# Writing the expert slots' results by token row instead of by slot row in a hybrid diffusion step

## Chip, cores and metric

The kernel is written for one Trainium2 chip and runs on one of its cores. The metric is the time of an execution on the device in microseconds (us); several executions are timed and the median is taken.

## What is computed

One layer of a diffusion backbone over 128 context and 512 latent tokens of width 1024, in fp32. A convolution branch and an mLSTM branch are merged, projected and added to the input. Then comes the part that this change is about, a mixture of experts:

```python
gl = x @ w_rg + b_rg                       # 4 groups: the top one is taken
el = (x @ w_re + b_re)[.., chosen group]   # 4 experts in it: the top two are taken
weights = gp_sel * topv                    # two weights per token
act = silu(x @ w_e_gate[e]) * (x @ w_e_up[e])      # 16 experts, 1024 -> 256
out[token] += weight * (act @ w_e_down[e])         # 256 -> 1024
x = x + gate2 * out;  y = rms_norm(x, norm_final_g)
```

The two results of a token are weighted and added after all experts have run.

## The kernel before

The 640 tokens are 5 tiles (`NT`) of 128 rows; with two experts each there are 1280 pairs of token and expert. The routing sorts the pairs into *slots* of 128 rows (`CAP`): slots 0 to 15 take the first 128 pairs of each expert, further slots what is left over, and the kernel runs an odd number of slots that it reads from the data (17 with these inputs). A slot that is not full has empty rows, whose token index lies outside the table, so that an indirect DMA skips them.

Each engine has its own instruction stream and they meet in semaphores. Matmuls take fp32 in two parts, a rounded high part and the rest (`_h`, `_l`), so every weight tile is halved once by ScalarE (ACT, high) and once by VectorE or GpSimd (low). For slot b the streams do the following; slots alternate between two sets of buffers s.

- SyncE (SP) loads the weights on its DMA queue: gate and up (1 MB each) of slot b+2 once TensorE has finished gate and up of slot b, and the down matrix (1 MB) of slot b+1 once the down product of b-1 is finished.
- ACT, function `slot`: high part of the activation of b-1, of x of b+1 (`x_high`), `store_y(s, b-2)`, high parts of gate and up of b+1 (L1516), silu of b, high part of the down matrix of b (L1511, semaphore `d_hi`), then the left half of the result of b-1 from PSUM into `yy` (L1560).
- VectorE (DVE): low part of the activation of b-1 and of x of b+1, low part of gate of b+1 (L1977), the product `act_` of b (L2021), low part of up of b+1 (L1977), right half of the result of b-1 into `yy` (L2002).
- TensorE (PE): turn `act_` of b-1 and the gathered x of b+1, gate and up of b, down of b-1, in this order.
- GpSimd (POOL), function `experts_pool`: for slot b the indirect DMA that gathers the x rows of slot b+3 (L609), then the low part of the down matrix of b (L631), which waits for `d_hi`. For b from 11 on the slot number comes from data: `counted_gather` first copies the column of indices to a fixed place, with a tiny operation (`carry`, L605) before and after the copy, and then issues the DMA.

The result of slot b leaves by `store_y`, a plain DMA of the whole tile on ACT's queue, to row b*128 of `y_d`. `y_left` and `y_right` of slot b wait on `y_st` until the store of b-2 has landed, because they write the same buffer. The rows of `y_d` that no slot may write are filled beforehand by ten plain copies of input on SP's queue (L689), early in the kernel. After the last slot POOL waits until all stores have landed and gathers for each of the 5 tiles the two rows of each token (`ya`, `yb`, L653, ten indirect DMAs by `row_i`). The last stage takes the tiles in order: ACT weighs `ya` (L1613), DVE adds the weighted `yb`, applies gate and residual and the final norm (L2045 to L2057), SP stores.

Of the kernel before, what the change touches and what calls it, by code (L numbers as in the profile page):

```python
# [10 lines left out]
P = 128  # L11
# [26 lines left out]
FILL = (NS - NE) // 2  # L38
# [117 lines left out]
def build(nc, a, out):  # L156
# [13 lines left out]
    y_d = nc.dram_tensor("y_d", [NS * CAP, D], F32, kind="Internal").ap()  # L170
# [114 lines left out]
    row_i = place("row_i", R0 + 3 * K + 64, [P, NT, 2], I32)  # L285
# [6 lines left out]
    ob = place("ob", 59 * K, [P, 2, NT, 2, NS], BF16)  # L292
# [16 lines left out]
    slot_b = place("slot_b", CV0 + 4 * K, [P, 2], I32)  # L309
    ah = place("ah", CV0 + 2 * K, [P, 2, P], F32R)  # L310
    al = place("al", CV0 + 3 * K, [P, 2, P], F32R)
    tick = place("tick", CV0 + 4 * K + 64, [P, 3], I32)
# [71 lines left out]
    picked, hots, slots, tables = sem("picked"), sem("hots"), sem("slots"), sem("tables")  # L384
    e_hi, e_lo, d_hi, d_lo, e_used = (sem(n) for n in ("e_hi", "e_lo", "d_hi", "d_lo", "e_used"))
    slot_set = sem("slot_set")
# [4 lines left out]
    y_act, y_dve = sem("y_act"), sem("y_dve")  # L391
# [92 lines left out]
    def routing(dve, then):  # L484
# [31 lines left out]
        dve.tensor_tensor(picks[:, :, :], full(13), full(14), ADD).then_inc(picked, 1)  # L516
# [43 lines left out]
        then(dve.tensor_copy(r1[:, 16, 0:2 * NS], psum[:, 6, 0:2 * NS]))  # L560
# [4 lines left out]
        then(dve.scalar_tensor_tensor(out=pair_of(6), in0=pair_of(2), scalar=float(CAP), in1=pair_of(4), op0=MUL, op1=ADD))  # L565
        dve.tensor_copy(row_i[:, :, :].rearrange("p t i -> p i t"), pair_of(6))
# [31 lines left out]
    def experts_pool(pool):  # L598
# [62 lines left out]
    def _(sp):  # L661
# [14 lines left out]
        for g in LOAD_ORDER:  # L676
# [54 lines left out]
        sp.wait_ge(y_st[0], 16 * FILL)  # L731
        sp.wait_ge(y_st[1], 16 * FILL)
# [11 lines left out]
        down_weights(0, 2 * pairs, by_table(2 * pairs), False)  # L744
        for t in range(NT):
# [48 lines left out]
    def _(pe):  # L794
# [351 lines left out]
        pe.wait_ge(picked, 1)  # L1146
# [9 lines left out]
        pe.wait_ge(hots, 1)  # L1156
        for n in range(2 * NT):
            mm = pe.matmul(psum[:, 6, 0:2 * NS], oa[:, n // NT, n % NT, :], ob[:, n // NT, n % NT, :, :],
                           start=(n == 0), stop=(n == 2 * NT - 1))
# [22 lines left out]
        def down(s, b, first=False):  # L1182
# [5 lines left out]
            if not first:  # L1188
                pe.wait_ge(y_act, b)
                pe.wait_ge(y_dve, b)  # L1190
# [37 lines left out]
    def _(act):  # L1228
# [326 lines left out]
        def y_left(s, j, b, first=False):  # L1555

            act.wait_ge(e_used, b + 1)
            if not first:
                act.wait_ge(y_st[s], 16 * (j + FILL))
            act.activation(yy[:, s, 0:512], psum[:, 5, :], ACT.Copy).then_inc(y_act, 1)  # L1560
# [10 lines left out]
        act.wait_ge(y_st[0], 16 * FILL)  # L1571
        act.wait_ge(y_st[1], 16 * FILL)
# [3 lines left out]
        def slot(b, s, u, last=False):  # L1576
# [7 lines left out]
            if early >= 2:  # L1584
                store_y(s, b - 2)
# [20 lines left out]
        store_y(1, 2 * pairs - 1)  # L1606
        y_left(0, pairs, 2 * pairs)
        store_y(0, 2 * pairs)
# [16 lines left out]
    def _(dve):  # L1625
# [460 lines left out]
```

## Time and profile before

| | us |
|---|---|
| median of 3 runs (lowest, highest) | 810.46 (809.5, 812.64) |
| the profiled execution: its own time | 812.8 |
| the profiled execution: span of its profile | 810.9 |
| mean granted TensorE clock over it | 0.942 of full speed |
| busy: PE, DVE, ACT, POOL | 686.9, 527.4, 348.0, 185.0 |

PE, PEld, DVE, ACT and POOL are the matmuls, the weight loads of TensorE, VectorE, ScalarE and GpSimd; ACTq and SPq are DMAs that ACT and SP issue. L12 is line 12 of the kernel. A row of the timeline gives start, duration, engine, line, operation, output<-input, and in brackets how long the engine was idle before it and what ended that. The span has these stretches: up to 578 us the layer's other parts and the routing, 585 to 768 us the 17 slots, 768 to 811 us the last stage.

### The profile page before, as it was taken

What the parts mean: (1) busy time and instruction counts of PE and PEld (TensorE: products, weight loads), DVE (VectorE), ACT (ScalarE), POOL (GpSimd) and SP (SyncE); (2) the same over time, 40 slices, a digit from 0 to 9 for tenths busy, and PEclk for the clock granted to TensorE, in tenths of its full rate; (3) what the DMA queues carried; (4) which work ended last, traced back from release to release, by engine and by line L of the source; (5) the groups of instructions that cost most, each with busy time, mean ns of one, the idle gap of its engine ahead of it and who ended that gap; (6) DMA issues with size and microseconds to landing.
All of it is one profiled execution on the core that took longest, in us unless ns stands there. A gap on an engine that the chain in (4) does not pass through costs nothing.

```text
span 810.9 us, 11103 instructions
## 1 busy us (share of the span) xinstructions
PE 686.9 (85%) x4391; PEld 608.7 (75%) x4391; DVE 527.4 (65%) x764; ACT 348.0 (43%) x467; POOL 185.0 (23%) x83
## 2 busy tenths in 40 slices
PE   2799999999888998899999999996189998989700
PEld 1599999999777888788889998884177777767600
DVE  2447999999376555633355554565857777788557
ACT  4542123433133343334375121036077767777432
POOL 3004222233000000000000000000147766797250
PEclk9889999999799999999999999998599999999955
DMA  9934144663305533623342436224299999999473
GB/s 318 349 108 144 53 156 158 233 232 108 107 14 113 103 32 105 121 90 104 104 152 90 138 103 232 78 106 157 96 315 366 367 367 380 395 391 374 160 272 122
DMA packets 80452, 150.22 MB, mean 185 GB/s; under 512 B 11669, under 2 KB 63217, under 8 KB 73713
## 3 DMA queue, kind: packets, MB, share of 16 engines
q1 hardware_dynamic: 62192, 121.25, 44.7%
q10 hardware_dynamic: 14320, 17.77, 6.6%
q0 software_dynamic: 3888, 10.49, 3.6%
q8 instruction: 35, 0.57, 0.3%
q14 instruction: 17, 0.13, 0.1%
HBM read 138.31 MB, written 20.09 MB: 195 GB/s over the span
## 4 chain that ended last, share of the span: by engine, by line
PE 40%; DVE 25%; POOL 11%; issue 9%; DMA 8%; ACT 5%; ACTq 2%; POOLq 0%; DVEq 0%
DVE psum L1714 13%; PE psum L843 13%; PE psum L1129 7%; POOL down_l L631 6%; PE psum L1087 4%; POOL xg L609 3%; PE psum L796 2%; DMA w_raw<-in_w_in 2%; PE psum L859 2%; PE psum L1020 1%; PE psum L939 1%; PE psum L986 1%; DMA cn<-in_state_n 1%; DMA xg<-h_d,slot_b 1%; DMA out_new_n<-cout 1%
## 5 line engine op out<-in xcount | busy, mean ns | idle before, releaser
L843 PE MATMUL psum<-hh,w_h 128*128 128x320 f32 x608 | 145.2, 320 | 2.9 <-ACT modrow L1403 1.9
L843 PE MATMUL psum<-hh,w_l 128*128 128x320 f32 x608 | 139.0, 310 | 0.0
L843 PE MATMUL psum<-hl,w_h 128*128 128x320 f32 x608 | 139.0, 310 | 0.0
L609 POOL DMA_INDIRECT xg<-h_d,slot_i x14 | 31.0, 2217 | 387.6 <-DVE slot_i L563 378.0
L1714 DVE SCALAR_TENSOR_TENSOR psum<-conv,taps,psum 128x760 f32<-128x760 f32 x106 | 107.6, 1015 | 3.6
L1977 DVE TENSOR_TENSOR w_l<-w_raw,w_h 128x2048 fp32r<-128x2048 f32 x34 | 94.9, 2794 | 19.8 <-ACT w_h L1516 19.8
L843 PEld LDWEIGHTS psum<-hh,w_h 128*128 128x128 f32 x608 | 100.2, 190 | 9.5 <-issue 6.4
L843 PEld LDWEIGHTS psum<-hl,w_h 128*128 128x128 f32 x608 | 102.3, 189 | 0.0
L843 PEld LDWEIGHTS psum<-hh,w_l 128*128 128x128 f32 x608 | 102.1, 189 | 0.0
L631 POOL TENSOR_TENSOR down_l<-down_raw,down_h 128x2048 fp32r<-128x2048 f32 x16 | 75.0, 4687 | 48.0 <-ACT down_h L1511 47.9
L788 POOL TENSOR_TENSOR w_l<-w_raw,w_h 128x2048 fp32r<-128x2048 f32 x9 | 41.7, 4637 | 150.2 <-ACT w_h L1234 150.2
L1516 ACT ACTIVATE w_h<-w_raw 128x2048 fp32r<-128x2048 f32 x34 | 65.2, 1923 | 18.4 <-DMA w_raw<-in_w_e_up 14.6
L1234 ACT ACTIVATE w_h<-w_raw 128x2048 fp32r<-128x2048 f32 x24 | 45.9, 1910 | 48.2 <-DMA w_raw<-in_w_in 31.2
L458 PE MATMUL psum<-w_h,xh 128*128 128x512 f32 x136 | 55.0, 405 | 0.0
L459 PE MATMUL psum<-w_h,xl 128*128 128x512 f32 x136 | 53.4, 393 | 0.0
L1511 ACT ACTIVATE down_h<-down_raw 128x2048 fp32r<-128x2048 f32 x17 | 32.6, 1916 | 24.2 <-DMA down_raw<-in_w_e_down 24.2
L1834 DVE TENSOR_TENSOR num<-psum,inter 128x129 f32<-128x129 f32 x32 | 9.4, 293 | 38.0 <-ACT inter L1322 38.0
L1868 DVE TENSOR_TENSOR w_l<-w_raw,w_h 128x2048 fp32r<-128x2048 f32 x13 | 29.6, 2281 | 6.3 <-ACT w_h L1234 6.3
L464 PE MATMUL psum<-w_l,xh 128*128 128x512 f32 x136 | 33.6, 389 | 0.0
L1322 ACT ACTIVATE inter<-psum,tokg 128x129 f32<-128x129 f32 x32 | 11.9, 371 | 50.5 <-PE psum L946 50.5
L1129 PE MATMUL psum<-w_h,mh 128*128 128x512 f32 x80 | 31.4, 393 | 1.1 <-DVE mrg L1929 1.1
L1129 PE MATMUL psum<-w_h,ml 128*128 128x512 f32 x80 | 31.2, 390 | 0.0
(335 smaller groups left out, 1314.6 us busy)
## 6 DMA issues: line engine op xcount, KB each, us to landing
w_raw<-in_w_ada SPq DMA_DIRECT2D x20, 1024.0 KB, 7.9
w_raw<-in_w_in SPq DMA_DIRECT2D x20, 1024.0 KB, 11.8
w_raw<-in_w_e_gate SPq DMA_DIRECT2D x17, 1024.0 KB
w_raw<-in_w_e_up SPq DMA_DIRECT2D x17, 1024.0 KB, 10.2
down_raw<-in_w_e_down SPq DMA_DIRECT2D x17, 1024.0 KB, 11.8
y_d<-yy ACTq DMA_DIRECT2D x17, 512.0 KB, 8.1
y_d<-in_x_sample SPq DMA_DIRECT2D x10, 512.0 KB, 7.5
w_more<-in_w_ada SPq DMA_DIRECT2D x4, 1024.0 KB, 11.9
```

What stands on the lines that cost most here:

```text
L458: pe.matmul(dst, lh, rh, start=(k == 0), stop=False)
L459: pe.matmul(dst, ll, rh, start=False, stop=False)
L464: mm = pe.matmul(dst, lh, rl, start=False, stop=(k == len(terms) - 1))
L609: pool.indirect_dma_start(out=xg[:, s, :], out_offset=None, in_=h2_d, in_offset=bass.IndirectOffsetOnAxis(ap=index, axis=0), bounds_check= ...
L631: pool.tensor_tensor(down_l[s][:, 0, :], down_raw[s][:, 0, :], down_h[:, s, :].bitcast(F32), SUB).then_inc(d_lo, 1)
L788: pool.tensor_tensor(w_l[:, g % RING, :], w_raw[:, g % RING, :], w_h[:, g % RING, :].bitcast(F32), SUB).then_inc(lo_done, 1)
L843: mm = pe.matmul(psum[:, p + q, 0:HALF], w, r[:, k, q * HALF:(q + 1) * HALF], start=(k == 0 and x == 0), stop=(k == KT - 1 and x == 2))
L1129: mm = pe.matmul(psum[:, n % 4, :], l, r, start=(k == 0 and x == 0), stop=(k == KT - 1 and x == 2))
L1234: act.activation(w_h[:, g % RING, :], w_raw[:, g % RING, :], ACT.Copy).then_inc(hi_done, 1)
L1516: act.activation(w_h[:, 2 * s + c, :], w_raw[:, 2 * s + c, :], ACT.Copy).then_inc(e_hi, 1)
L1714: ins = dve.scalar_tensor_tensor(out=after, in0=src, scalar=w, in1=before, op0=MUL, op1=ADD)
L1977: dve.tensor_tensor(w_l[:, 2 * s + c, :], w_raw[:, 2 * s + c, :], w_h[:, 2 * s + c, :].bitcast(F32), SUB).then_inc(e_lo, 1)
```

## The change

`y_d` becomes a table of 2*640 rows: row i*640 + token holds the result for the token's i-th expert. The routing makes a second table, `pair_i`, beside the one for the gather: per slot and row the row of `y_d`. It comes from a third plane of `ob` in the same matmuls (78 instead of 52 columns). `store_y` is gone; POOL scatters the rows of slot b-2 by indirect DMA, between its gather of b+3 and its low part of b. The ten filling copies and the waits on them are gone. The last stage's ten indirect gathers become ten plain loads on SP's queue, after POOL has seen all scatters land. The semaphores of the two halves of a result become one (`y_out`).

```diff
@@ routing, DVE @@
+        dve.tensor_scalar(ob[:, 1, :, 2, :], obh[:, 1, :, :], float(NT), None, MUL)
...
-        then(dve.tensor_copy(r1[:, 16, 0:2 * NS], psum[:, 6, 0:2 * NS]))
+        then(dve.tensor_copy(r1[:, 16, 0:3 * NS], psum[:, 6, 0:3 * NS]))
...
-        then(dve.scalar_tensor_tensor(out=pair_of(6), in0=pair_of(2), scalar=float(CAP), in1=pair_of(4), op0=MUL, op1=ADD))
-        dve.tensor_copy(row_i[:, :, :].rearrange("p t i -> p i t"), pair_of(6))
+        then(dve.scalar_tensor_tensor(out=r1[:, 6, 0:NS], in0=r1[:, 16, 2 * NS:3 * NS], scalar=float(P), in1=r1[:, 17, 0:NS],
+                                      op0=MUL, op1=ADD))
+        dve.tensor_scalar(pair_i[:, :], r1[:, 6, 0:NS], float(EMPTY * P), None, ADD)
@@ experts_pool @@
+        def scatter(s, index):
+
+            pool.indirect_dma_start(out=y_d, out_offset=bass.IndirectOffsetOnAxis(ap=index, axis=0), in_=yy[:, s, :],
+                                    in_offset=None, bounds_check=2 * T - 1, oob_is_err=False).then_inc(y_st[s], 16)
+
+        def known_scatter(b):
+
+            pool.wait_ge(y_out, 2 * b + 2)
+            scatter(b % 2, pair_i[:, b:b + 1])
+
+        def counted_scatter(s, b):
+
+            pool.wait_ge(y_out, 2 * b + 2)
+            carry(2, pair_i[:, 0:1])
+            pool.tensor_copy(pair_b[:, s:s + 1], pair_i[:, bass.ds(b, 1)]).then_inc(pair_set, 1)
+            pool.wait_ge(pair_set, b - (POOL_LOOP_AT - 3))
+            carry(3, pair_b[:, s:s + 1])
+            scatter(s, pair_b[:, s:s + 1])
...
         for b in range(POOL_LOOP_AT):
             known_gather(b + 3)
+            if b >= 2:
+                known_scatter(b - 2)
             low(b % 2, b)
...
                 counted_gather(1 - s, b + 3)
+                counted_scatter(s, b - 2)
                 low(s, b)
         counted_gather(0, 2 * pairs)
+        counted_scatter(1, 2 * pairs - 5)
         low(1, 2 * pairs - 3)
+        counted_scatter(0, 2 * pairs - 4)
         low(0, 2 * pairs - 2)
+        counted_scatter(1, 2 * pairs - 3)
         low(1, 2 * pairs - 1)
-        pool.wait_ge(y_st[0], 16 * (pairs + 1 + FILL))
-        pool.wait_ge(y_st[1], 16 * (pairs + FILL))
-        carry(2, row_i[:, 0, 0:1])
-        for t in range(NT):
-            for i, buf in enumerate((ya, yb)):
-                pool.indirect_dma_start(out=buf[:, t, :], out_offset=None, in_=y_d,
-                                        in_offset=bass.IndirectOffsetOnAxis(ap=row_i[:, t, i:i + 1], axis=0),
-                                        bounds_check=NS * CAP - 1).then_inc(yg_in[t], 16)
+        counted_scatter(0, 2 * pairs - 2)
+        counted_scatter(1, 2 * pairs - 1)
+        counted_scatter(0, 2 * pairs)
+        pool.wait_ge(y_st[0], 16 * (pairs + 1))
+        pool.wait_ge(y_st[1], 16 * pairs)
+        pool.tensor_tensor(tick[:, 0:1], pair_i[:, 0:1], pair_i[:, 0:1], ADD).then_inc(y_all, 1)
@@ SP @@
-            n = g - 2 * NRAW_ADA
-            if 0 <= n < NS - NE:
-                sp.dma_start(y_d[(NE + n) * CAP:(NE + n + 1) * CAP, :],
-                             a["x_sample"][0, (n % (NT - 1)) * P:(n % (NT - 1) + 1) * P, :]).then_inc(y_st[n % 2], 16)
...
+        sp.wait_ge(y_all, 1)
+        for t in range(NT):
+            for i, buf in enumerate((ya, yb)):
+                sp.dma_start(buf[:, t, :], y_d[i * T + t * P:i * T + (t + 1) * P, :]).then_inc(yg_in[t], 16)
@@ ACT @@
-        def store_y(s, b):
-            act.wait_ge(y_act, b + 1)
-            act.wait_ge(y_dve, b + 1)
-            rows = slice(b * CAP, (b + 1) * CAP) if isinstance(b, int) else bass.ds(b * CAP, CAP)
-            act.dma_start(y_d[rows, :], yy[:, s, :]).then_inc(y_st[s], 16)
...
-            if early >= 2:
-                store_y(s, b - 2)
...
-        store_y(1, 2 * pairs - 1)
         y_left(0, pairs, 2 * pairs)
-        store_y(0, 2 * pairs)
```

## Rows read from the trace of the kernel before

**Rows 1.** The page: GB/s in 40 slices of 20.3 us.

```profile
GB/s 318 349 108 144 53 156 158 233 232 108 107 14 113 103 32 105 121 90 104 104 152 90 138 103 232 78 106 157 96 315 366 367 367 380 395 391 374 160 272 122
```

**Rows 2.** The page, DMA queues: packets, MB, share of 16 engines.

```profile
...
q10 hardware_dynamic: 14320, 17.77, 6.6%
q0 software_dynamic: 3888, 10.49, 3.6%
```

**Rows 3.** Waits between 610 and 737 us: total, times, longest.

```profile
...
ACT down_h L1511 <- DMA down_raw<-in_w_e_down: 19.2, 12, 2.1
PEld psum L796 <- DVE act L2021: 14.0, 10, 2.2
```

**Rows 4.** Windows: busy of PE, PEld, DVE, ACT, POOL; clock, DMA share, GB/s.

```profile
...
623.20:634.50 11.30, 9.53 (x47) 7.76 (x46) 8.22 (x7) 7.66 (x9) 7.51 (x3) 1.00 1.00 395
634.50:644.50 10.00, 9.62 (x48) 7.83 (x47) 8.13 (x7) 7.70 (x9) 7.55 (x3) 1.00 0.94 352
```

**Rows 5.** Timeline, slots with fixed numbers, POOL, DVE and ACT.

```profile
...
609.77 4.72 POOL L631 TENSOR_TENSOR down_l<-down_raw,down_h 128x2048 fp32r<-128x2048 f32 x1 [5.00 <-ACT down_h L1511]
...
684.52 4.62 POOL L631 TENSOR_TENSOR down_l<-down_raw,down_h 128x2048 fp32r<-128x2048 f32 x1 [2.54 <-ACT down_h L1511]
688.00 3.29 DVE L1977 TENSOR_TENSOR w_l<-w_raw,w_h 128x2048 fp32r<-128x2048 f32 x1 [1.01 <-ACT w_h L1516]
689.30 2.88 POOL L609 DMA_INDIRECT xg<-h_d,slot_i  x1 [0.16 <-issue]
691.22 0.41 DVE L2021 TENSOR_TENSOR act<-psum,sil 128x256 f32<-128x256 f32 x1
691.55 2.28 DVE L1977 TENSOR_TENSOR w_l<-w_raw,w_h 128x2048 fp32r<-128x2048 f32 x1
692.87 1.92 ACT L1511 ACTIVATE down_h<-down_raw 128x2048 fp32r<-128x2048 f32 x1 [1.85 <-DMA down_raw<-in_w_e_down]
...
694.88 4.62 POOL L631 TENSOR_TENSOR down_l<-down_raw,down_h 128x2048 fp32r<-128x2048 f32 x1 [2.70 <-ACT down_h L1511]
...
705.21 4.62 POOL L631 TENSOR_TENSOR down_l<-down_raw,down_h 128x2048 fp32r<-128x2048 f32 x1 [2.67 <-ACT down_h L1511]
```

**Rows 6.** Timeline, slots with counted numbers, POOL, DVE and PE.

```profile
...
720.37 2.25 POOL L605 TENSOR_TENSOR tick<-slot_i 128x1 int32<-128x1 int32 x1
722.56 0.18 POOL L623 COPY slot_b<-slot_i 128x1 int32 x1
722.82 2.33 POOL L605 TENSOR_TENSOR tick<-slot_b 128x1 int32<-128x1 int32 x1
725.30 1.05 POOL L609 DMA_INDIRECT xg<-h_d,slot_b  x1 [0.15 <-issue]
726.39 4.66 POOL L631 TENSOR_TENSOR down_l<-down_raw,down_h 128x2048 fp32r<-128x2048 f32 x1
728.78 4.43 DVE L1977 TENSOR_TENSOR w_l<-w_raw,w_h 128x2048 fp32r<-128x2048 f32 x1 [1.17 <-ACT w_h L1516]
...
737.01 4.65 POOL L631 TENSOR_TENSOR down_l<-down_raw,down_h 128x2048 fp32r<-128x2048 f32 x1
...
742.61 1.07 PE L464 MATMUL psum<-down_l,ah 128*128 128x512 f32 x4
```

**Rows 7.** Timeline from the last result on.

```profile
...
767.66 0.69 DVE L2002 COPY yy<-psum 128x512 f32<-128x512 f32 x1 [1.39 <-PE psum L464]
...
771.36 0.19 POOL L605 TENSOR_TENSOR tick<-row_i 128x1 int32<-128x1 int32 x1 [10.24 <-DMA y_d<-yy]
772.14 1.05 POOL L653 DMA_INDIRECT ya<-y_d,row_i  x1 [0.59 <-issue]
...
778.75 1.15 ACT L1613 ACTIVATE ya<-ya,wgt 128x1024 f32<-128x1024 f32 x1 [10.51 <-DMA yb<-y_d,row_i]
```

**Rows 8.** DMA issues: count, KB each, median us to landing.

```profile
...
y_d<-yy ACTq DMA_DIRECT2D x17, 512.0 KB, 8.1
x<-in_x_prompt SPq DMA_DIRECT2D x1, 512.0 KB, 3.4
```

**Rows 9.** Timeline of the routing, DVE.

```profile
...
576.63 0.35 DVE L553 TENSOR_SCALAR ob<-obh,tokcol 128x260 bf16<-128x260 f32 x1
```

More of the change, by code:

```diff
@@ L37 @@
 NS = NB + NB % 2
-FILL = (NS - NE) // 2
 EMPTY = 16
@@ L169, in build @@
     mod2_d = nc.dram_tensor("mod2_d", [2, 4 * D], F32, kind="Internal").ap()
-    y_d = nc.dram_tensor("y_d", [NS * CAP, D], F32, kind="Internal").ap()
+    y_d = nc.dram_tensor("y_d", [2 * T, D], F32, kind="Internal").ap()
     ident = keep("ident", [P, P])
@@ L284, in build @@
     wgt = place("wgt", R0 + 3 * K, [P, NT, 2])
-    row_i = place("row_i", R0 + 3 * K + 64, [P, NT, 2], I32)
+    pair_i = place("pair_i", R0 + 3 * K + 256, [P, NS], I32)
     slot_i = place("slot_i", R0 + 3 * K + 128, [P, NS], I32)
@@ L291, in build @@
     oa = place("oa", 56 * K, [P, 2, NT, P], BF16)
-    ob = place("ob", 59 * K, [P, 2, NT, 2, NS], BF16)
+    ob = place("ob", 59 * K, [P, 2, NT, 3, NS], BF16)
     obh = place("obh", 62 * K, [P, 2, NT, NS])
@@ L309, in build @@
     slot_b = place("slot_b", CV0 + 4 * K, [P, 2], I32)
+    pair_b = place("pair_b", CV0 + 4 * K + 32, [P, 2], I32)
     ah = place("ah", CV0 + 2 * K, [P, 2, P], F32R)
     al = place("al", CV0 + 3 * K, [P, 2, P], F32R)
-    tick = place("tick", CV0 + 4 * K + 64, [P, 3], I32)
+    tick = place("tick", CV0 + 4 * K + 64, [P, 4], I32)
     bg2 = place("bg2", R0 + 5 * K, [P, 2, D])
@@ L383, in build @@
     rt_x, rt_exp, rt_pe = sem("rt_x"), sem("rt_exp"), sem("rt_pe")
-    picked, hots, slots, tables = sem("picked"), sem("hots"), sem("slots"), sem("tables")
+    hots, slots, tables = sem("hots"), sem("slots"), sem("tables")
     e_hi, e_lo, d_hi, d_lo, e_used = (sem(n) for n in ("e_hi", "e_lo", "d_hi", "d_lo", "e_used"))
-    slot_set = sem("slot_set")
+    slot_set, pair_set = sem("slot_set"), sem("pair_set")
     xg_in = [sem(f"xg_in{i}") for i in range(2)]
@@ L390, in build @@
         sem(n) for n in ("gu_done", "sil_done", "act_done", "at_done", "a_hi", "a_lo"))
-    y_act, y_dve = sem("y_act"), sem("y_dve")
+    y_out, y_all = sem("y_out"), sem("y_all")
     y_st = [sem(f"y_st{i}") for i in range(2)]
@@ L515, in routing @@
                                    plane(hot, GE).unsqueeze(2).to_broadcast([P, NT, NG, GE]), MUL))
-        dve.tensor_tensor(picks[:, :, :], full(13), full(14), ADD).then_inc(picked, 1)
+        dve.tensor_tensor(picks[:, :, :], full(13), full(14), ADD).then_inc(hots, 1)
         dve.wait_ge(rt_pe, 1)
@@ L730, in _ @@
         sp.wait_ge(h2_st, 16 * NT)
-        sp.wait_ge(y_st[0], 16 * FILL)
-        sp.wait_ge(y_st[1], 16 * FILL)
         down_weights(0, 0, own(0), True)
@@ L1144, in _ @@
         mm.then_inc(lg_done, 1)
-        pe.wait_ge(picked, 1)
+        pe.wait_ge(hots, 1)
         for t in range(NT):
@@ L1154, in _ @@
         mm.then_inc(rt_pe, 1)
[L1156 to L1159, printed above, removed]
+        pe.wait_ge(hots, 2)
+        for i in (1, 0):
+            for t in range(NT):
+                mm = pe.matmul(psum[:, 6, 0:(2 + i) * NS], oa[:, i, t, :], ob[:, i, t, 0:2 + i, :],
+                               start=(i == 1 and t == 0), stop=(i == 0 and t == NT - 1))
         mm.then_inc(rt_pe, 1)
@@ L1188, in down @@
             if not first:
-                pe.wait_ge(y_act, b)
-                pe.wait_ge(y_dve, b)
+                pe.wait_ge(y_out, 2 * b)
             for q in range(2):
@@ L1558, in y_left @@
             if not first:
-                act.wait_ge(y_st[s], 16 * (j + FILL))
-            act.activation(yy[:, s, 0:512], psum[:, 5, :], ACT.Copy).then_inc(y_act, 1)
-        def store_y(s, b):
-            act.wait_ge(y_act, b + 1)
-            act.wait_ge(y_dve, b + 1)
-            rows = slice(b * CAP, (b + 1) * CAP) if isinstance(b, int) else bass.ds(b * CAP, CAP)
-            act.dma_start(y_d[rows, :], yy[:, s, :]).then_inc(y_st[s], 16)
+                act.wait_ge(y_st[s], 16 * j)
+            act.activation(yy[:, s, 0:512], psum[:, 5, :], ACT.Copy).then_inc(y_out, 1)
         for q in range(2):
@@ L1570, in _ @@
         act.wait_ge(h2_st, 16 * NT)
-        act.wait_ge(y_st[0], 16 * FILL)
-        act.wait_ge(y_st[1], 16 * FILL)
         load_mod(act, 3, bg2, gate2_in)
@@ L2000, in y_right @@
             if not first:
-                dve.wait_ge(y_st[s], 16 * (j + FILL))
-            dve.tensor_copy(yy[:, s, 512:D], psum[:, 6, :]).then_inc(y_dve, 1)
+                dve.wait_ge(y_st[s], 16 * j)
+            dve.tensor_copy(yy[:, s, 512:D], psum[:, 6, :]).then_inc(y_out, 1)
         for c in range(2):
```

## The prediction, made before the change was run

> **What bounds the kernel now.** I read the page first, for where the DMA engines are full, then the queues and the waits of the expert slots, then one slot after the other in the timeline, and the last stage row by row. In the expert slots the DMA rate stands at 366 to 395 GB/s for seven slices in a row, against less than 235 GB/s in nearly every slice before it [rows 1]. So bytes saved there can be worth time, and bytes saved elsewhere (the ten filling copies, early in the kernel) are not: I cost their removal at nothing, because the slices in which they run (102 to 175 us, the sixth to ninth) carry 156 to 233 GB/s.
>
> A slot moves 3 x 1.05 MB of weights, a store of 0.524 MB and the gathered rows. That empty rows move no bytes can be read off the software queue: its 10.49 MB are 2560 rows of 4 KB, exactly two rounds of the 1280 real rows (x once, results once), while its 3888 packets are 27 indirect DMAs of 128 + 16 [rows 2]. An empty row costs a packet and no data. So the gather is 5.24/17 = 0.31 MB a slot, the slot 3.98 MB, and at 375 GB/s, the middle of the slices, 10.6 us. POOL's work on the down matrix comes once a slot; nine periods from 609.77 to 705.21 are 10.60 us each [rows 5]. The two agree, and ACT waits for weights in every slot [rows 3].
>
> But DMA is not alone there. PE has 9.5 us of work in a slot of 11.3 [rows 4], and it waits for the product `act_` of DVE [rows 3], which stands behind DVE's low part of the gate weights. That row takes 3.29 us where the like one after it takes 2.28, since POOL holds something that both need: POOL's 4.62 us on the down matrix end at 689.14, and DVE's operation, begun at 688.00, ends 2.15 us after that. The same holds the other way round: the gather issued at 689.30 takes 2.88 us and ends 0.9 us after DVE's [rows 5], while one that meets no such operation takes 1.05 [rows 6]. So POOL's and DVE's big subtractions exclude each other, and an indirect DMA cannot begin inside DVE's. The slots alternate between long ones, with DMA share 1.00, and short ones of about 10 us with 0.94 [rows 4]: DMA ends the wait in the one, this chain nearly does in the other.
>
> **Part 1, fixed slots (2 to 10): the bytes.** The stores go from 17 x 0.524 = 8.91 MB to 5.24 MB, 3.67 MB less, 9.8 us of DMA time at 375 GB/s or 0.58 us a slot. The slot's DMA time falls from 10.6 to 10.0 us. Nine periods: at most -5.4 us.
>
> **Part 2, fixed slots: the scatter on POOL.** In the row order of one slot, from the start T of the down operation: it ends at T+4.62; DVE's gate part runs to T+6.77; the gather, blocked by it, ends at T+7.66 (684.52 to 692.18). `act_` takes DVE to T+7.0, and the up part runs from T+7.03 to T+9.3 [rows 5]. Now the scatter is queued behind the gather. It wants to start at T+7.8, inside the up part, so it is held until T+9.3 and ends 0.9 later, at T+10.2; the next down operation starts at T+10.36. Today that operation starts at T+10.36 as well (694.88), let go by ACT's `down_h`, which waited for DMA [rows 5]. So the scatter fits, but it sets a floor: low part, gate part, `act_`, up part and scatter in a ring give 10.36 us. The trace has no scatter; its bounds are 1.05 us (free) and 2.88 (blocked), and I take the blocked one, as the gather in the same place. The period goes from 10.60 to 10.4: 9 x 0.2 = -2 us. If the long slots stay long, because a load's latency and not the rate makes them, nothing is gained and the short ones lose 0.1: +0.7.
>
> At this place the Trainium skill speaks against the change: its page SBUF — State Buffer, section "Who interferes with whom", has software-made DMAs (POOL's) share a port with DVE that DMAs of ACT and SP do without, and a store is moved from the second kind to the first. The gather's 2.88 us against 1.05 agrees. The same section infers that a two-input DVE operation holds up only POOL's reads, so that the making of descriptors would go on beside it; by that the floor would be gone (a rival below).
>
> **Part 3, counted slots (11 to 13).** Here POOL has no gap: the two tiny operations take 2.25 and 2.33 us because each ends with a DVE weight operation, the copy 0.18 and the gather 1.05; the down operation of one slot follows that of the last after 10.6 us without idle time [rows 6]. The counted scatter adds a tiny operation (0.19 when nothing blocks it, as the one at 771.36 [rows 7]), the copy 0.18, another 0.19, gaps of 0.3 and 1.05 for the DMA: 1.9 us free, and up to 2.3 more for each tiny operation that meets DVE. It comes when DVE works from PSUM, before its next gate part (728.78, 2.4 us after the down operation's start [rows 6]), so I take 1.9. Three times that is 5.7 us. What is late next: the down operation of slot 13, which ends at 741.67 and which PE's last pass of down needs at 742.61 [rows 6]. That cover is 0.9 us, so PE is late by 4.8. Behind it on POOL stand the last gathers, late by 3.8 after two scatters, which fits under the same delay. Afterwards POOL has idle gaps for the other scatters. +4.8 us; the low end is +2 (the tiny operations of the gather are then blocked for a shorter time, because DVE is ahead), the high end +9.
>
> **Part 4, the end.** Today the last result is in `yy` at 768.35, the store, POOL's tiny operation and two gathers follow, and ACT starts on the first tile at 778.75: 10.4 us [rows 7]. Afterwards: tiny operation, copy, tiny operation and gaps 0.9; the scatter from issue to landing between 1.05 + 2.8 = 3.9 (the plain store took 2.8 to 771.36) and 5.3 (two gathers issued 1.3 us apart took 6.6 to 778.75 [rows 7]), 4.3 since the last slot holds few rows; POOL's signal to SP 0.5; two plain loads of 0.5 MB, of which one took 3.4 us [rows 8] and the second adds up to 1.4: 4.2. Sum 9.9, so -0.5 us, with bounds -1.6 and +1.5. The ten loads are 5.2 MB, 2.8 us a tile at 375 GB/s. I cost them at nothing after the first tile, since the DVE operations and not the gathers pace the tiles today; without that cover they would show as waits of ACT.
>
> **Part 5, small ones.** The third plane of `ob` is one more DVE operation before the first gather, half the size of the one of 0.35 us [rows 9]: 0.25, and the wider copy 0.05. +0.3 us, on the path. `pair_i` costs what `row_i` did. ACT loses 17 DMA issues, each beside other work: nothing. The renamed semaphores: nothing. The fifteen first scatters must land before `yy` is written again: a store of this size lands in 8.1 us [rows 8], and a scatter issued at T+7.8, held for 1.5 us, has until about T+20 us. Hidden, by some 2 us.
>
> **Sum.** -2.0 + 4.8 - 0.5 + 0.3 = +2.6 us. The profiled execution had its own time 812.8 us (span 810.9, 1.9 around it), so 815.4 on its scale; it lies 2.3 above the median 810.46 of the runs shown, so the median should be 813.1. Within 0.5% (4.05 us) a measurement of this kernel can hardly tell a change, so this is "no change", on its upper side. By itself this case reaches from 809.5 to 816.
>
> **Rivals.**
> *Slower: the counted scatter meets DVE's lock* (0.22). If in slots 11 to 13 one tiny operation of each scatter falls into DVE's gate or up part, it costs 2.2 us more, 3 x 2.2 = 6.6 at most, of which I expect most: 819. For it: every tiny operation in that loop today meets one [rows 6]. Against it: the scatter comes behind both weight operations. It decides from a scatter section of 2.4 us instead of 1.9, since then DVE's gate part is there first.
> *Slower: scatters land late* (0.10). Behind the gather in the same queue, with all DMA engines busy, the scatter could take 11 us and more. Then ACT and DVE wait to write `yy`, and everything after them in ACT's order (the high parts) is late. Past 10 us to landing each of 12 slots would lose up to 0.5: 816 to 819. For it: the cover is thin. Against it: a plain store took 8.1 [rows 8].
> *No lock for the scatter* (0.12). Then part 2 has no floor and the period falls to the 10.0 us of DMA: -5.4 + 4.8 - 0.5 + 0.3 = -0.8, 809.7. This is what the inference of the Trainium skill's page SBUF — State Buffer, section "Who interferes with whom", would give. Against it: the gather was held.
> *Faster: the bytes decide everywhere* (0.13). Full relief in the fixed slots, -5.4, the counted slots at their low end, +2, the tail at its low end, -1.6, and +0.3: -4.7, 805.8. It decides once the fixed period is under 10.1 and POOL's added time in the counted slots under 2 us a chain. For it: DMA share near 1 in the long slots [rows 4]. Against it: POOL without a gap in the counted ones [rows 6].
> The forecast keeps 0.43. That the change doesn't remove the bytes I exclude by the software queue's count.
>
> **Chances.** Faster by over 0.5%: the faster rival 0.13, and 0.03 from the edges of the forecast and the no-lock case: 0.16. Slower: 0.22 + 0.10, and 0.09 from the forecast's upper edge: 0.41. The rest, 0.43. The range 806 to 819 leaves out about one in ten on either side.
>
> **What the profile would show.** The software queue at 3888 packets or near and 10.49 MB, and 17.77 - 8.91 = 8.9 MB in the queue that held the stores. In slots 2 to 10, a period of 10.4 us and scatter rows of about 2.9, ending 0.9 us after a DVE weight operation. In slots 11 to 13, down operations 12 to 12.5 us apart, and PE waiting for POOL's `down_l` in slot 14. From the last `yy` to ACT's first tile 9.9 us. What would make it wrong: a landing time of the scatter far from 8 us, a scatter whose work on POOL grows with something that the gather's does not, or DVE and POOL falling into another order once POOL is late, as each slot's order is a race of about 1 us.

## The result, and the profile of the changed kernel

The changed kernel has a median of 818.48 us (8 executions, 811.33 to 821.61) beside 810.21 us (8 executions, 807.69 to 813.89) for the kernel before on the same chip: a ratio of 1.0091, 95% interval 1.0057 to 1.0124. That is slower by 0.9%, about 7.4 us, more than the 0.5% below which no change can be told. The ratio, here and below, is estimated from the undisturbed executions of both kernels and is not exactly the quotient of the medians beside it, which are over all executions (here they stand 8.3 us apart). The profiled execution took 815.61 us, with a span of 813.8; since it lies 2.9 us under its median and the profiled one of before 2.6 over its own, the two spans differ by only 2.9 us. So I read them stretch by stretch and not by their ends.

Busy tenths of POOL in 40 slices (20.3 us each), from the page of the kernel before:

```profile
POOL 3004222233000000000000000000147766797250
```

The page of the changed kernel: busy tenths of POOL and GB/s in 40 slices, and the DMA queues; they answer to [rows 1, 2].

```profile
POOL 3004222233000000000000000000269999999700
...
GB/s 317 348 105 145 52 104 108 170 140 104 107 19 107 118 44 81 179 86 100 153 60 167 123 28 233 104 78 155 141 354 364 368 352 346 371 271 348 107 266 123
...
q10 hardware_dynamic: 11872, 8.86, 3.8%
q0 software_dynamic: 4896, 10.50, 3.5%
```

The bytes did go: 8.86 MB stay in the queue that held the stores, 17.77 before. The rate in the expert slots fell as well, from a range of 366 to 395 GB/s to one of 346 to 371 with one slice of 271, and POOL is busy for 90% or more in seven slices in a row, before in one. The DMA engines have been relieved, and POOL has become the busy one.

POOL in nine slots with fixed numbers: groups of its instructions (count, busy us, mean ns, idle time before them and what ended it). The first list is of before and has the down operations of slots 1 to 9, the second is of after and has those of slots 1 to 10.

```profile
L631 POOL TENSOR_TENSOR down_l<-down_raw,down_h 128x2048 fp32r<-128x2048 f32 x9 | 41.7, 4631 | 28.8 <-ACT down_h L1511 28.8
```

```profile
L652 POOL TENSOR_TENSOR down_l<-down_raw,down_h 128x2048 fp32r<-128x2048 f32 x10 | 46.6, 4659 | 1.7 <-ACT down_h L1534 1.5
...
L632 POOL DMA_INDIRECT y_d<-yy,pair_i x9 | 21.9, 2432 | 2.8 <-issue 2.8
```

Of the 28.8 us for which POOL stood still before, 5.0 stand ahead of slot 1's operation, and the 2.67 ahead of slot 10's aren't among them [rows 5]; so between the starts of the two POOL waited 26.5 us for ACT. After, 1.3 of the 1.5 us stand ahead of slot 1's operation, and POOL waited 0.24 us in the nine slots. The scatter with its gap (21.9 + 2.8) ate the slack. One such slot of after, POOL and DVE, which answers to [rows 5]:

```profile
679.63 4.63 POOL L652 TENSOR_TENSOR down_l<-down_raw,down_h 128x2048 fp32r<-128x2048 f32 x1
684.42 2.90 POOL L611 DMA_INDIRECT xg<-h_d,slot_i  x1 [0.16 <-issue]
687.63 2.30 POOL L632 DMA_INDIRECT y_d<-yy,pair_i  x1 [0.31 <-issue]
689.95 4.62 POOL L652 TENSOR_TENSOR down_l<-down_raw,down_h 128x2048 fp32r<-128x2048 f32 x1
```

```profile
682.90 3.53 DVE L1988 TENSOR_TENSOR w_l<-w_raw,w_h 128x2048 fp32r<-128x2048 f32 x1 [1.00 <-ACT w_h L1539]
...
686.76 2.28 DVE L1988 TENSOR_TENSOR w_l<-w_raw,w_h 128x2048 fp32r<-128x2048 f32 x1
```

DVE's up part ends at 689.04 and the scatter at 689.93, 0.9 us later, as the gather does after the gate part (686.43 and 687.32). The down operation follows at once.

The slots with counted numbers on POOL, which answer to [rows 6]:

```profile
705.35 2.25 POOL L607 TENSOR_TENSOR tick<-slot_i 128x1 int32<-128x1 int32 x1
707.54 0.18 POOL L625 COPY slot_b<-slot_i 128x1 int32 x1
707.80 2.33 POOL L607 TENSOR_TENSOR tick<-slot_b 128x1 int32<-128x1 int32 x1
710.27 1.06 POOL L611 DMA_INDIRECT xg<-h_d,slot_b  x1
711.36 0.20 POOL L607 TENSOR_TENSOR tick<-pair_i 128x1 int32<-128x1 int32 x1
711.49 0.19 POOL L644 COPY pair_b<-pair_i 128x1 int32 x1
711.76 0.19 POOL L607 TENSOR_TENSOR tick<-pair_b 128x1 int32<-128x1 int32 x1
712.49 1.02 POOL L632 DMA_INDIRECT y_d<-yy,pair_b  x1 [0.54 <-issue]
713.54 4.58 POOL L652 TENSOR_TENSOR down_l<-down_raw,down_h 128x2048 fp32r<-128x2048 f32 x1
...
726.31 6.00 POOL L652 TENSOR_TENSOR down_l<-down_raw,down_h 128x2048 fp32r<-128x2048 f32 x1
...
737.65 2.82 POOL L632 DMA_INDIRECT y_d<-yy,pair_b  x1 [0.54 <-issue]
740.50 4.55 POOL L652 TENSOR_TENSOR down_l<-down_raw,down_h 128x2048 fp32r<-128x2048 f32 x1
```

The down operations stand 12.8 (700.77 to 713.54), 12.8 and 14.2 us apart, 10.6 before. The scatter section takes 2.2 us (711.36 to 713.54). The third distance is longer since one down operation met DVE's weights (6.00 us) and one scatter did (2.82). The three together are 39.7 us, 7.9 more than before. In slots 14 and 15 the scatters' tiny operations meet DVE too (2.25 us at 745.01, 2.25 and 2.33 from 753.82 on), but before the change POOL was idle for 4.3 and 5.7 us there, and PE waits 0.24 us for slot 15's operation and not at all for slot 14's.

What PE waited for between 705 and 768 us, from the waits (total, times, longest), first before, then after; from the down operation of slot 10 to the last `yy` the numbers are the same:

```profile
PE psum L796 <- DVE act L2021: 2.2, 3, 1.0
PE psum L796 <- DMA xg<-h_d,slot_b: 1.7, 2, 1.5
...
PE psum L458 <- DVE al L1994: 1.2, 1, 1.2
```

```profile
PE psum L464 <- POOL down_l L652: 5.2, 4, 3.1
PE psum L819 <- DVE act L2032: 2.9, 3, 1.3
PE psum L458 <- DVE al L2005: 1.3, 1, 1.3
```

PE's waits are 5.1 us before and 9.4 after, and the new one is for POOL's `down_l`, four times (1.55, 0.31, 3.13 and 0.24 us, for slots 11, 12, 13 and 15). The second thing is what PE does behind such waits. Timeline of PE, after:

```profile
718.18 1.21 PE L464 MATMUL psum<-down_l,ah 128*128 128x512 f32 x4 [1.55 <-POOL down_l L652]
720.68 0.70 PE L819 MATMUL psum<-ident,act 128*128 128x128 f32 x2 [1.28 <-DVE act L2032]
...
724.16 0.63 PE L459 MATMUL psum<-w_h,xl 128*128 128x512 f32 x1
724.59 0.63 PE L458 MATMUL psum<-w_h,xh 128*128 128x512 f32 x1
...
726.65 0.39 PE L459 MATMUL psum<-w_h,xl 128*128 128x512 f32 x1
726.88 0.39 PE L458 MATMUL psum<-w_h,xh 128*128 128x512 f32 x1
```

After two waits of 1.55 and 1.28 us the matmuls begin 0.43 us apart, until 726.3, and then 0.23 apart: TensorE's clock stood at the lower level, 1.2 GHz, instead of 2.4. The windows (last three columns: granted clock, DMA share, GB/s) give its mean in the stretch, first before, then after:

```profile
713.50:726.30 12.80, 10.33 (x51) 8.32 (x50) 10.85 (x10) 10.46 (x13) 12.39 (x7) 1.00 0.97 385
...
759.80:772.60 12.80, 6.47 (x27) 4.55 (x25) 4.43 (x5) 3.66 (x5) 1.97 (x3) 0.97 0.21 84
```

```profile
713.50:726.30 12.80, 9.96 (x37) 7.79 (x35) 11.52 (x8) 9.49 (x10) 11.86 (x10) 0.74 0.91 333
...
759.80:772.60 12.80, 10.45 (x38) 7.75 (x36) 4.43 (x5) 3.65 (x5) 9.08 (x9) 0.87 0.22 87
```

The loss in a window is its length times what the clock lacks of 1.00, less what falls into a wait. The first window gives 12.8 x 0.26 = 3.3 us. In windows of 1 us the lower level stands from 719.7 to 726.5, so 1.0 us of it lies in the wait that ends at 720.68, and 2.8 us are lost. The second window gives 12.8 x 0.13 = 1.7 us (lower level from 767.5 to 770.9). The 0.97 of before counts for nothing: the clock falls only at about 771.8, behind its last `yy` at 768.35.

Between the down operation of slot 10 and the last `yy` lie 63.1 us before (705.21 to 768.35) and 71.8 after (700.77 to 772.58): 8.7 us more. The waits give 4.3 of them and the clock 4.5, together 8.8. The same reckoning fits all twelve profiles of this case: that stretch less PE's waits and less the loss by the clock is 57.3 to 58.8 us in each.

The end, which answers to [rows 7]:

```profile
771.89 0.69 DVE L2013 COPY yy<-psum 128x512 f32<-128x512 f32 x1 [2.67 <-PE psum L464]
...
773.93 1.00 POOL L632 DMA_INDIRECT y_d<-yy,pair_b  x1 [0.54 <-issue]
776.63 0.18 POOL L680 TENSOR_TENSOR tick<-pair_i 128x1 int32<-128x1 int32 x1 [1.71 <-DMA y_d<-yy,pair_b]
...
777.22 0.43 SPq L767 DMA_DIRECT2D yb<-y_d  x1
...
781.69 1.15 ACT L1624 ACTIVATE ya<-ya,wgt 128x1024 f32<-128x1024 f32 x1 [9.30 <-DMA yb<-y_d]
```

From the last `yy` (772.58) to ACT's first tile are 9.1 us, 10.4 before. From there to the end are 32.1 us in both. The last scatter needs 2.7 us from issue to landing, and ACT starts 4.5 us after the issue of the second load (777.22).

### The profile page after: what moved, and what is told of

The parts are those of the page before. It is cut to its first block, busy times and chain, and to the rows that moved or that the text cites. A ratio compares the mean times of both kernels' runs of the same rounds, so it can differ in the third digit from the quotient of the medians.

```text
span 813.8 us, 11100 instructions
## 1 busy us (share of the span) xinstructions
PE 691.2 (85%) x4391; PEld 611.9 (75%) x4391; DVE 535.2 (66%) x765; ACT 348.2 (43%) x467; POOL 218.5 (27%) x114
## 3 DMA queue, kind: packets, MB, share of 16 engines
q10 hardware_dynamic: 11872, 8.86, 3.8%
q0 software_dynamic: 4896, 10.50, 3.5%
HBM read 133.07 MB, written 14.85 MB: 182 GB/s over the span
## 4 chain that ended last, share of the span: by engine, by line
PE 38%; DVE 25%; POOL 12%; issue 10%; DMA 7%; ACT 5%; ACTq 2%; POOLq 0%; SPq 0%; DVEq 0%
PE psum L866 14%; DVE psum L1725 13%; PE psum L1152 7%; PE psum L1110 4%; POOL down_l L652 4%; POOL xg L611 3%; POOL y_d L632 3%; PE psum L819 2%; POOL tick L607 2%; PE psum L962 2%; PE psum L882 1%; DMA w_raw<-in_w_in 1%; PE psum L1043 1%; PE psum L1009 1%; DMA down_raw<-in_w_e_down 1%
## 5 line engine op out<-in xcount | busy, mean ns | idle before, releaser
L611 POOL DMA_INDIRECT xg<-h_d,slot_i x14 | 33.1, 2364 | 385.0 <-DVE slot_i L564 375.5
L1988 DVE TENSOR_TENSOR w_l<-w_raw,w_h 128x2048 fp32r<-128x2048 f32 x34 | 103.2, 3037 | 16.3 <-ACT w_h L1539 16.3
L1539 ACT ACTIVATE w_h<-w_raw 128x2048 fp32r<-128x2048 f32 x34 | 65.0, 1925 | 14.6 <-DMA w_raw<-in_w_e_up 13.2
L1879 DVE TENSOR_TENSOR w_l<-w_raw,w_h 128x2048 fp32r<-128x2048 f32 x13 | 29.6, 2282 | 8.4 <-ACT w_h L1257 8.4
L1345 ACT ACTIVATE inter<-psum,tokg 128x129 f32<-128x129 f32 x32 | 11.9, 371 | 49.3 <-PE psum L969 49.3
## 6 DMA issues: line engine op xcount, KB each, us to landing
w_more<-in_w_ada SPq DMA_DIRECT2D x4, 1024.0 KB, 11.9
```

The source lines that it names most:

```text
L611: pool.indirect_dma_start(out=xg[:, s, :], out_offset=None, in_=h2_d, in_offset=bass.IndirectOffsetOnAxis(ap=index, axis=0), bounds_check= ...
L1539: act.activation(w_h[:, 2 * s + c, :], w_raw[:, 2 * s + c, :], ACT.Copy).then_inc(e_hi, 1)
L1988: dve.tensor_tensor(w_l[:, 2 * s + c, :], w_raw[:, 2 * s + c, :], w_h[:, 2 * s + c, :].bitcast(F32), SUB).then_inc(e_lo, 1)
```

## The experiments

The theory: the counted scatter lengthens POOL's chain in slots 11 to 13 and that is the loss; the fixed slots gain almost nothing because POOL and DVE, by turns, are as slow as the full stores were. Rivals: the scatters themselves cost time wherever they stand; the filling copies or the routing did it; the pair of traces misleads. Ratios are to the kernel before on the same chip, with 95% intervals. In the table "fixed" is the mean distance of down operations over nine slots, "counted" the next three distances, "to yy" the time from the down operation of slot 10 to the last `yy`, "tail" from there to ACT's first tile, all in us from the one profile of each; the last column is the ratio of the times.

| kernel | fixed | counted | to yy | tail | ratio |
|---|---|---|---|---|---|
| before | 10.60 | 10.6, 10.6, 10.6 | 63.1 | 10.4 | 1 |
| after | 10.50 | 12.8, 12.8, 14.2 | 71.8 | 9.1 | 1.0091 |
| e1_nofill | 10.42 | 10.6, 10.6, 10.4 | 64.2 | 10.3 | 1.0016 |
| e2_store80 | 10.11 | 10.5, 10.6, 10.6 | 62.6 | 10.5 | 0.9933 |
| e3_b_fixed17 | 10.47 | 10.4, 10.4, 11.7 | 64.1 | 10.2 | 0.9972 |
| e4_a_fixed17 | 10.50 | 10.2, 10.2, 10.8 | 62.7 | 8.5 | 0.9962 |
| e5_after_again | 10.55 | 12.8, 14.6, 10.9 | 70.9 | 9.2 | 1.0082 |
| e6_counted_gather | 10.46 | 11.7, 12.0, 11.9 | 71.8 | 8.4 | 1.0042 |
| e7_empty_scatters | 10.55 | 10.2, 10.6, 10.5 | 62.9 | 10.6 | 0.9970 |
| e8_copy_once | 10.49 | 12.2, 10.5, 10.6 | 64.2 | 8.6 | 0.9987 |
| e9_store80_fixed17 | 10.23 | 10.4, 10.0, 10.2 | 63.3 | 10.3 | 0.9863 |
| e10_store80_empty | 10.39 | 10.2, 10.2, 10.4 | 61.7 | 10.5 | 0.9939 |

**e1_nofill.** The kernel before without the filling copies; the last gathers name only the 17 slots' rows.

```diff
-                sp.dma_start(y_d[(NE + n) * CAP:(NE + n + 1) * CAP, :], ...).then_inc(y_st[n % 2], 16)
-                ... indirect_dma_start(out=buf[:, t, :], out_offset=None, in_=y_d,
+                ... indirect_dma_start(out=buf[:, t, :], out_offset=None, in_=y_d[0:(NE + 1) * CAP, :],
```

> The kernel before without the ten early filling copies; the last gathers read only the 17 slots' rows of y_d. My theory: the copies were hidden, so 0 (within 1 us of before, 810.2). Rival: their removal is what brought the first expert gather of the changed kernel 2.3 us earlier in its profile (577.44 against 579.71), then about -2 us.

809.2 beside 808.87 us: 1.0016 (0.998 to 1.0052). The copies were hidden, as costed.

**e2_store80.** The kernel before with stores of 80 rows instead of 128. It leaves out rows of the result; the other 48 rows of each slot are filled early, by copies that the extract doesn't show.

```diff
-            rows = slice(b * CAP, (b + 1) * CAP) if isinstance(b, int) else bass.ds(b * CAP, CAP)
-            act.dma_start(y_d[rows, :], yy[:, s, :]).then_inc(y_st[s], 16)
+            rows = slice(b * CAP, b * CAP + 80) if isinstance(b, int) else bass.ds(b * CAP, 80)
+            act.dma_start(y_d[rows, :], yy[0:80, s, :]).then_inc(y_st[s], 16)
```

> The kernel before with each slot's store cut to its first 80 rows (this leaves out rows of the result; the rows not stored are filled early), about the bytes that the change leaves, but still on ACT's queue and with no new work on POOL. Theory that bytes bound the slots: the fixed slots go from 10.6 to 10.0 or 10.2 us, -4 us there and -1 to -2 behind, 805 in all. Rival, that load latency and PE and not bytes set the pace: 0 to -1, 809 to 810.

803.78 us, 0.9933 (0.9895 to 0.9971), and 10.11 us a fixed slot. So the bytes alone are worth 0.67%, 5.4 us, of which the fixed slots give 9 x 0.49 = 4.5: fewer bytes do shorten them, and part 1 was sized right. In the changed kernel the same slots gain 0.9 us; e10_store80_empty asks whether POOL's turn takes the rest.

**e3_b_fixed17 and e4_a_fixed17.** The kernels before and after with the slot count written into POOL's stream, so that every gather and scatter is a fixed one (right only for 17 slots). For the one after:

```diff
-        with pool.Fori(POOL_LOOP_AT // 2, pairs - 2) as p:
-            ... counted_gather, counted_scatter, low ...
+        for b in (11, 12, 13):
+            known_gather(b + 3)
+            known_scatter(b - 2)
+            low(b % 2, b)
+        for b in (14, 15):
+            known_scatter(b - 2)
+            low(b % 2, b)
+        for b in (14, 15, 16):
+            known_scatter(b)
```

> The kernel before with POOL's stream written out for the 17 slots that these inputs have, so no counted gathers with their tiny operations. Theory: POOL is just in time before the change, so little is gained: 0 to -2 us, 808 to 810.

> The changed kernel with POOL's stream written out for 17 slots, so neither counted gathers nor counted scatters. My theory, that the change loses its time on POOL in the counted slots: last ten slots in 63 to 65 us instead of 71.8, 809 to 811 in all, 8 below the changed kernel. Rival, that the scatters land late or that scattered writes are slow: still 815 or more.

0.9972 (0.9935 to 1.0009) and 0.9962 (0.9933 to 0.9992). The change without its counted operations is faster than the kernel before by 0.4%, with them slower by 0.9%: the counted part costs 1.3%, about 10.5 us, and there the change loses. 806.2 us is less than the 809 to 811 that I expected. Like for like, e4_a_fixed17 beside e3_b_fixed17 (807.84 us), the change brings 0.1% by the ratios, which is no difference that can be told: the kernel before may lose 0.3% by its own counted gathers. In its slots 11 to 13 the scatter takes 2.2 to 2.8 us on POOL without the tiny operations.

**e5_after_again.** The changed kernel once more, no edit, for a second profile.

> The changed kernel once more, beside the others of this call. 8 us slower than before, as in the first comparison, and a profile in which the down operations of slots 10 to 13 are 12.8 us or more apart.

816.64 beside 811.73 us: 1.0082 (1.005 to 1.0114). In its profile POOL and DVE meet in another order (12.8, 14.6, 10.9), and the third distance isn't the 12.8 or more that I expected, but up to the last `yy` there are again 7.8 us more than before. PE waits 11.0 us in the stretch, 5.9 more than before, and the clock stands at the lower level from 730.2 to 733.6, which loses 1.7 us. Waits and clock give 7.6.

**e6_counted_gather.** The changed kernel with fixed scatters and counted gathers.

```diff
+        for b in (11, 12, 13):
+            counted_gather((b + 3) % 2, b + 3)
+            known_scatter(b - 2)
+            low(b % 2, b)
...
```

> The changed kernel with POOL's stream written out for 17 slots, where the gathers of slots 14 to 16 keep their tiny operations and copies and all scatters go by fixed columns. Theory, that POOL's time in a counted slot is what counts: a scatter adds 1.1 us there instead of 2.2, three of them 3.3, less the 0.9 of cover, so about 2.4 above the kernel with everything fixed (which was 0.4% below before): 0 to -1 against before, 7 or 8 below the changed kernel. Rival, that any scatter there upsets the order between DVE and POOL and costs the same: at least 5 above before.

814.88 us, 1.0042 (1.001 to 1.0075): neither theory's number. The period there is

```profile
712.93 4.64 POOL L652 TENSOR_TENSOR down_l<-down_raw,down_h 128x2048 fp32r<-128x2048 f32 x1
717.53 2.24 POOL L607 TENSOR_TENSOR tick<-slot_i 128x1 int32<-128x1 int32 x1
719.72 0.18 POOL L625 COPY slot_b<-slot_i 128x1 int32<-128x1 int32 x1
719.98 2.33 POOL L607 TENSOR_TENSOR tick<-slot_b 128x1 int32<-128x1 int32 x1
722.47 1.06 POOL L611 DMA_INDIRECT xg<-h_d,slot_b  x1 [0.15 <-issue]
723.84 1.02 POOL L632 DMA_INDIRECT y_d<-yy,pair_i  x1 [0.31 <-issue]
```

that is 11.95 us to the next down operation at 724.88. The chain of before had no gap in these slots [rows 6], so even a free scatter of 1.02 us and its gap of 0.31 lengthens each. I had reckoned from e4_a_fixed17, where the gather had lost its tiny operations too. With a scatter behind them, the counted gathers cost 0.8% (1.0042 less 0.9962, and the intervals don't overlap). What the scatter's own copy and tiny operations add is at most 0.4% (1.0082 less 1.0042) and not shown: the intervals overlap, and the medians, 816.64 and 814.88 us, are 0.2% apart. This profile doesn't tell them apart either: up to the last `yy` it takes 71.8 us, as that of the changed kernel, with 9.6 us of PE's waits (3.1 of them for DVE's low part of the weights, 1.1 for POOL's `down_l`) and 3.4 us lost at the lower clock.

**e7_empty_scatters.** e3_b_fixed17 with one more indirect DMA at each place where the change has a scatter in slots 2 to 15, all 128 of its indices outside its table.

```diff
+            if b >= 2:
+                empty_scatter()    # indices none_i: all 3 * T, bounds_check 2 * T - 1
```

> The kernel before with POOL's stream written out for 17 slots and, at the places of the change's scatters, an indirect DMA whose 128 indices all lie outside the table, so that it moves nothing; the stores stay on ACT's queue. It has POOL's work of the change without its saving of bytes. Theory: the ring of 10.4 us stays under the DMA's 10.5, so 0 to +3 us against the same kernel without them (0.3% below before). Rival, that each scatter costs its 2.2 us on the path: +20 and more.

0.997 (0.994 to 1.0), the same as without them. While the stores are full, no cost of an indirect DMA more per slot on POOL can be told (10.55 us a fixed slot, 10.47 without). It takes as long as one that moves rows, here 2.25 us, in the next slot 2.70:

```profile
617.43 2.25 POOL L633 DMA_INDIRECT none_d<-x,none_i  x1 [0.30 <-issue]
```

**e8_copy_once.** The changed kernel for any slot count, with the index columns of the last slots copied once while POOL is idle, and two columns in each copy of the loop.

```diff
+        pool.tensor_copy(last_i[:, 0:1], slot_i[:, bass.ds(2 * pairs, 1)]).then_inc(last_set, 1)
+        pool.tensor_copy(last_i[:, 1:7], pair_i[:, bass.ds(2 * pairs - 5, 6)]).then_inc(last_set, 1)
...
+                    pool.tensor_copy(slot_b[:, :], slot_i[:, bass.ds(b + 3, 2)]).then_inc(slot_set, 1)
+                    pool.tensor_copy(pair_b[:, :], pair_i[:, bass.ds(b - 2, 2)]).then_inc(pair_set, 1)
```

> The changed kernel for any number of slots, but the index columns of the last slots are copied to a fixed place once, early, while POOL is idle, and those of the two slots of a loop iteration in one go; a tiny operation stays before each indirect DMA to hold its wait. Theory: the second slot of the loop and the slots behind it lose most of their extra POOL time: between the kernel with everything fixed (-0.4%) and before, 807 to 810 where before is 809. Rival: as the changed kernel, +5 or more.

810.6 us beside 811.73 for before and 816.64 for after: 0.9987 (0.9953 to 1.0022). The loss is gone, a gain over before can't be told. Only the loop's first distance is still long (12.2); one tiny operation of 2.24 to 2.25 us, one of 1.3 at most and two DMAs fit in 10.6 us.

**e9_store80_fixed17 and e10_store80_empty.** The short stores together with the fixed gathers, without and with the empty DMAs; they ask whether POOL's turn takes back what the bytes bring. Both leave out rows of the result, as e2_store80 does.

```diff
# e9: the edits of e2_store80 and e3_b_fixed17;  e10: those of e7_empty_scatters too
```

> The kernel before with POOL's stream written out for 17 slots and stores cut to 80 rows (rows of the result are left out; they are filled early): the bytes saved, no scatter. Both theories: fixed slots at about 10.1 us, total 0.7 to 1.0% below before.

> The same with the indirect DMAs that move nothing at the places of the scatters (again with rows of the result left out). My theory, that the ring of POOL and DVE keeps the saved bytes from becoming time: fixed slots back at 10.4 to 10.5 us, 3 us of the gain gone, 0.4 to 0.6% below before. Rival, that the bytes saved by the change are eaten by slower scattered writes and not by the ring: fixed slots stay at 10.1.

798.22 us (6 executions), 0.9863 (0.9821 to 0.9904), and 804.52 us, 0.9939 (0.9908 to 0.997). With the bytes gone, the kernel with the same empty DMAs that cost nothing in e7_empty_scatters is slower by 0.76%, 6.3 us. The second came out as expected, the first did not: it is 1.4% below before instead of 0.7 to 1.0, and its fixed slots take 10.23 us, not 10.1. In e10_store80_empty POOL goes round without a wait:

```profile
615.26 4.65 POOL L640 TENSOR_TENSOR down_l<-down_raw,down_h 128x2048 fp32r<-128x2048 f32 x1
620.07 2.90 POOL L612 DMA_INDIRECT xg<-h_d,slot_i  x1 [0.16 <-issue]
623.27 2.21 POOL L633 DMA_INDIRECT none_d<-x,none_i  x1 [0.31 <-issue]
625.51 4.64 POOL L640 TENSOR_TENSOR down_l<-down_raw,down_h 128x2048 fp32r<-128x2048 f32 x1
```

That is 10.25 us a round, the ring of part 2 (forecast 10.36) seen bare; the mean of 10.39 comes from one round of 11.1, whose empty DMA took 3.12 us. But the two profiles differ in the fixed slots by only 9 x 0.16 = 1.4 us, and from slot 10 to the last `yy` e10_store80_empty is 1.6 us the shorter. Of the 4.6 us between the two spans, 4.2 stand ahead of the first gather (571.1 and 575.3 us), where the kernels differ by one small operation of the routing. So the ring is seen in the rows and in the length of the fixed slots; that it is worth the whole 6 us is not shown.

## Why it came out slower

The direction was not forecast: "no change, on its upper side" had 0.43, slower 0.41. The mechanisms were right for the most part, one term was too small, and one was missing. That 818.48 us lies within 806 to 819 is partly luck: the forecast by itself reached to 816, and the 819 at the upper end was priced for two other mechanisms, neither of which did it.

**Fixed slots (parts 1 and 2).** Right. Forecast 10.4 us a slot, -2 us in all; measured 10.50, -0.9. The bytes are worth about what part 1 said (e2_store80: 0.49 us a fixed slot, forecast 0.58), and the ring of POOL and DVE takes most of it: with the scatters or the empty DMAs, POOL is never idle and a slot takes 10.50 and 10.39 us, without them 10.11 (e2_store80) and 10.23 (e9_store80_fixed17). Scatter rows of 2.2 to 2.6 us were forecast as 2.9, although the prediction's own working (from T+7.8 to T+10.2) has 2.4.

**Counted slots (part 3).** This is the step that failed in size: "Three times that is 5.7 us ... PE is late by 4.8" was 8.7, and 7.8 in the second profile. The place, POOL's unbroken chain and PE's wait for `down_l` in slot 14 (3.1 us at 745.11) were as forecast. The scatter section took 2.2 instead of 1.9, and the distances 12.8 and 14.2 instead of 12 to 12.5, as later ones meet DVE, so the chain grew by 7.9 us (6.5 in the second profile) and not by 5.7. The cover of 0.9 us, read at slot 13, was not one: in slot 11 it was 0.5 (POOL done at 720.41, PE's pass at 720.90), and there PE waited for `down_l` already, 1.55 us.

And a term was missing: PE's clock fell behind two of its stalls. For the clock I have rows, not an experiment. It is 1.00 from slot 10 to the last `yy` in the profiles of before, e2_store80, e4_a_fixed17, e7_empty_scatters, e9_store80_fixed17 and e10_store80_empty, and that stretch takes 61.7 to 63.3 us there. In e1_nofill, e3_b_fixed17 and e8_copy_once some 3.4 us stand at the lower level, a loss of 1.7, and the stretch takes 64.1 to 64.2, though none of these is slower than before in its median by anything that could be told. So such a fall isn't the change's alone. It accounts for half of the excess of the first profile, and for a fifth of the second's.

**The end (part 4).** Forecast -0.5, measured -1.3 (10.4 to 9.1), mainly since the last scatter landed in 2.7 us and not 4.3. **The routing (part 5).** From the routing's logits to the operation that writes the index table 14.85 us before, 15.19 after: +0.34, forecast +0.3.

With these, -0.9 + 8.7 - 1.3 + 0.3 = +6.8 us, beside 8.3 between the medians and 7.4 by the ratio. The two spans differ by less (2.9) because the first gather starts at 577.4 us instead of 579.7, and over all profiles it lies between 571 and 580 with no relation to any edit that I can see; and because slot 1's down operation follows slot 0's after 9.6 us instead of 11.4. That 11.4 belongs to this one profile: in all eleven others, those made from the kernel before too, it is 9.4 to 9.6.

**The software queue.** I forecast 3888 packets; there are 4896, 34 indirect DMAs of 144. That was a slip of counting: 17 gathers and 17 scatters, where before it was 17 and 10.

**The rivals.** *The counted scatter meets DVE's lock*, priced at 819, is nearest in time but not in mechanism: the tiny operations of the scatter were free in all three slots (0.20 us), while the scatter's DMA (2.82) and a down operation (6.00) met DVE. They did meet DVE in slots 14 and 15, where POOL had been idle and PE waited only 0.24 us for it. *Scatters land late*: the condition came true and the cost did not. The scatters of the fixed slots took 11.3 us to land, past the 10 of the rival, and the room was 11.9 us (issued at 687.63, the buffer written again at 699.56); there is one wait of ACT for it, 0.64 us. *No lock for the scatter* is refuted, by 2.2 us and more in every fixed slot of the changed kernel. By the Trainium skill's page SBUF — State Buffer, section "Who interferes with whom", the making of descriptors would go on beside a two-input DVE operation, as it infers; the rows have the scatter held all the same, and they decide on its time. They don't show what is held: the scatter also reads its 128 indices from a tile in SBUF, and the same section has such an operation hold up POOL's reads. *The bytes decide everywhere* comes near only without a scatter (10.11 us a fixed slot in e2_store80, 10.23 in e9_store80_fixed17).

**Open.** Two profiles of the changed kernel show two orders of POOL and DVE, which fits a race, but what each order costs wasn't measured. Its executions spread from 811 to 822 both times; those of before from 808 to 814 the first time, but from 806 to 822 beside e5_after_again, so a wider spread is not shown. Nor was the clock's share tried by itself, nor what makes the clock fall: the longest wait, 3.13 us before 745.11, was not followed by a fall. Where the 6 us between e9 and e10 come from stays open too.

## What to carry to other kernels

Before moving work to an engine because it stands idle on average, look at each stretch: here POOL had 26.5 us of slack in nine slots and none in the next three, and the same scatter cost nothing that could be told in the ones, while in the others the change lost its time. A resource that is relieved gives its gain only down to the next limit, here a ring of two engines that shut each other out, 10.25 us beside 10.6; find the ring's length first. Index handling that depends on data belongs where the engine is idle, not in its tightest loop.

## What the runs showed of the hardware

- An indirect DMA whose 128 indices are all outside the table took 2.2 to 3.1 us on POOL where it was issued beside DVE's subtraction (e7_empty_scatters, e10_store80_empty), as one that moves rows (2.2 to 3.1). It took 1.01 us in the one slot where it began before DVE's operation (669.65 and 670.05 in e7_empty_scatters); one that moves rows and meets none took 1.02. So its price on POOL does not come from the rows that it moves.
- A scatter issued beside busy DMA engines landed after 11.3 us (median of the nine in the fixed slots), those of slots 9 to 16 after 4.9 (median of eight), and the last one, with nothing beside it, after 2.7.
- TensorE's granted clock stood at the lower level (matmuls 0.43 instead of 0.23 us apart) from 719.7 to 726.5 us; a wait of 1.55 us, 1.2 us of matmuls and the first 0.3 us of a wait of 1.28 us stood before the fall. A wait of 3.31 us stood before the fall in e5_after_again, but one of 3.13 us in the changed kernel's first profile had no fall behind it, so the length of the last wait alone does not decide.
